# Differential queries' transpose stored and loaded from ScalarE's queue, head outputs reloaded one step later

## What is computed

```python
for l in range(2):
    h = rms_norm(x, norm_gain)
    proj = h @ w_in                       # q, k, v, z of both kinds, and two gates
    # 8 differential heads (DA): q, k are normed and rotated first
    a  = softmax(mask(q1 @ k1.T)) - lam * softmax(mask(q2 @ k2.T))
    ua = rms_norm(a @ va) * (1 - lambda_init) * silu(da_z)
    # 16 stick-breaking heads (SB), two at a time
    w  = exp(log_sigmoid(z) + after)      # after: a reversed cumulative sum
    ub = (w @ vs) * silu(sb_z)
    y  = sigmoid(gate_a) * (ua @ w_branch_a) + sigmoid(gate_b) * (ub @ w_branch_b)
    x  = x + y @ w_out
x = second_block(x, ...)                  # two more layers, not touched here
```

## Time and profile before

| what | us |
|---|---|
| median of 3 runs | 3225.98 |
| range of the runs | 3220.62 to 3230.3 |
| the profiled execution, its own time | 3236.04 |
| span of its instructions | 3234.3 |
| PE busy | 3181.7 |
| DVE busy | 2051.8 |
| ACT busy | 1668.3 |

### The profile page before, as it was taken

The page is one execution under the profiler, slowest core; times in us unless marked ns, Lnnn a source line. Parts: engine busy times, 40 slices in busy tenths (PEclk is TensorE's granted clock), DMA queues, the critical chain, the costliest instruction groups (busy, mean ns, idle before and its releaser), DMA issues.

```text
span 3234.3 us, 46398 instructions
## 1 busy us (share of the span) xinstructions
PE 3181.7 (98%) x16602; PEld 2725.8 (84%) x16602; DVE 2051.8 (63%) x2347; ACT 1668.3 (52%) x2326; POOL 516.5 (16%) x425
## 2 busy tenths in 40 slices
PE   9999999999999999999999999999999999999999
PEld 7877878887888888778778888888889999999997
DVE  6766755555544455666655555544458888688975
ACT  5444455565444444454455555544446557465663
POOL 4635500000000003446420000000001000200000
PEclk9999999999999999999999999999999999999999
DMA  7656566666555555666566666665564444544454
GB/s 254 206 192 204 188 213 215 201 203 213 191 193 195 192 194 190 207 205 204 197 205 206 207 203 204 200 194 194 193 209 161 162 141 148 180 162 161 147 180 146
DMA packets 203372, 619.32 MB, mean 191 GB/s; under 512 B 22672, under 2 KB 57632, under 8 KB 202848
## 3 DMA queue, kind: packets, MB, share of 16 engines
q1 hardware_dynamic: 201760, 608.35, 58.1%
q0 software_dynamic: 1488, 9.26, 0.8%
HBM read 590.26 MB, written 27.26 MB: 191 GB/s over the span
## 4 chain that ended last, share of the span: by engine, by line
PE 73%; DMA 12%; DVE 5%; issue 4%; ACT 3%; SPq 3%; POOL 1%; ACTq 0%; DVEq 0%; POOLq 0%
PE acc L2042 15%; PE acc L2044 15%; PE acc L2043 15%; PE acc L2399 5%; PE acc L2400 5%; PE acc L2401 5%; DMA qk_moved<-QB 4%; DMA u_moved<-UB 4%; DMA UT<-u_moved 2%; DVE w_lo L1249 2%; DMA QL<-qk_moved 2%; ACT w_hi L732 2%; SPq L485 1%; DVE QB L1378 1%; SPq L495 1%
## 5 line engine op out<-in xcount | busy, mean ns | idle before, releaser
L1249 DVE TENSOR_TENSOR w_lo<-raw,w_hi 128x1024 fp32r<-128x1024 f32 x1055 | 1378.2, 1317 | 936.4 <-ACT w_hi L732 801.0
L732 ACT ACTIVATE w_hi<-raw 128x1024 fp32r<-128x1024 f32 x831 | 869.8, 1056 | 831.6 <-PE acc L2044 811.0
L2042 PE MATMUL acc<-w_hi,hT_hi 128*128 128x512 f32 x2560 | 1012.7, 396 | 13.7 <-DVE w_lo L1249 12.2
L2043 PE MATMUL acc<-w_lo,hT_hi 128*128 128x512 f32 x2560 | 999.3, 390 | 0.0
L2044 PE MATMUL acc<-w_hi,hT_lo 128*128 128x512 f32 x2560 | 999.2, 390 | 0.0
L2042 PEld LDWEIGHTS acc<-w_hi,hT_hi 128*128 128x128 f32 x2560 | 482.7, 189 | 117.9 <-DVE w_lo L1249 16.0
L2044 PEld LDWEIGHTS acc<-w_hi,hT_lo 128*128 128x128 f32 x2560 | 482.3, 188 | 102.4
L2043 PEld LDWEIGHTS acc<-w_lo,hT_hi 128*128 128x128 f32 x2560 | 482.9, 189 | 97.3
L746 ACT ACTIVATE w_hi<-raw 128x1024 fp32r<-128x1024 f32 x224 | 236.1, 1056 | 260.3 <-PE acc L2401 200.3
L2399 PE MATMUL acc<-h_hi,w_hi 128*128 128x272 f32 (+1 forms) x1088 | 318.5, 293 | 0.0
L2400 PE MATMUL acc<-h_lo,w_hi 128*128 128x272 f32 (+1 forms) x1088 | 311.9, 287 | 0.0
(11 more groups left out here) (377 smaller groups left out, 3764.3 us busy)
## 6 DMA issues: line engine op xcount, KB each, us to landing
raw<-weights SPq DMA_DIRECT2D x1056, 512.0 KB, 4.0
qk_moved<-QB SPq DMA_DIRECT2D x32, 512.0 KB, 4.3
QL<-qk_moved SPq DMA_DIRECT2D x128, 128.0 KB, 3.1
u_moved<-UB SPq DMA_DIRECT2D x32, 256.0 KB, 3.7
UT<-u_moved SPq DMA_DIRECT2D x128, 64.0 KB, 2.6
mat<-mats POOLq DMA_DIRECT2D x2, 1536.0 KB, 8.8
X<-x_in SPq DMA_DIRECT2D x8, 256.0 KB, 7.6
GB_rows<-rows POOLq DMA_DIRECT2D x1, 2048.0 KB, 10.8
```

The source lines that it names most:

```text
L732: act.activation(w_hi[:, slot, :], raw[:, slot, :], ACT.Copy).then_inc(hi_ready, 1)
L1249: dve.tensor_tensor(w_lo[:, s % RING, :], raw[:, s % RING, :], w_hi[:, s % RING, :], ALU.subtract)\
L2042: pe.matmul(o, stat[0][:, kc, token], hi, start=(kc == 0), stop=False)
L2043: pe.matmul(o, stat[0][:, kc, token], lo, start=False, stop=False)
```

## The change

Three things change.

1. For DA heads, the store to `qk_moved` and the loads into `QL` are issued by ACT and no more by SP. On ACT the store stands behind half 3, `evac_vz` follows, and the four loads stand between it and half 4. DVE's transpose into `QB` moves ahead of half 1 (it stood ahead of half 2).
2. For SB pairs, the store and the loads stay on SP. The four loads into `QL` move from behind half 16's weight load to the end of the step.
3. The output of a head is still stored in the step in which it is made, but its four loads into `UT`, `u_hi` and `u_lo` move into the following step: on SP behind the weight load of half 7, on ACT behind half 4, on DVE behind half 5. A step therefore gets a third argument, `done`, the head before `prev`, and the first loop turn of each kind is written out. The last head of a layer is handled behind the steps.

```diff
-                step(kind_of(l, i, "SB"), kind_of(l, i - 1, "SB"))
-            step(None, kind_of(l, 7, "SB"))
+                step(kind_of(l, i, "SB"), kind_of(l, i - 1, "SB"), kind_of(l, i - 2, "SB"))
+            step(None, kind_of(l, 7, "SB"), kind_of(l, 6, "SB"))
...
+        def load_qk(eng, m):
+            eng.wait_ge(qk_stored, 16 * (m["n"] + 1))
+            for j in range(4):
+                eng.dma_start(QL[32 * j:32 * j + 32, :, :, :].rearrange("p i b r -> p i (b r)"),
...
# SP
-                loads(first, 4, 6)
-                if prev["kind"] == "DA":
-                    store_qk(prev)
-                loads(first, 6, 7)
-                if prev["kind"] == "DA":
-                    load_qkT(prev)
-                loads(first, 7, 16)
+                loads(first, 4, 8)
+                if done:
+                    load_uT(done)
+                loads(first, 8, 16)
                 if this and this["kind"] == "SB":
-                    store_qk(this)
-                loads(first, 16, 17)
+                    store_qk(sp, this)
+                loads(first, 16, 17 + late)
+                store_u(prev)
+                loads(first, 17 + late, 20)
                 if this and this["kind"] == "SB":
-                    load_qkT(this)
-                loads(first, 17, 17 + late)
-                store_u(prev)
-                loads(first, 17 + late, 18 + late)
-                load_uT(prev)
-                loads(first, 18 + late, 20)
+                    load_qk(sp, this)
...
# ACT
-                if prev:
-                    split(u, 0, 4)
-                    evac_vz(prev)
+                split(u, 0, 4)
                 if prev["kind"] == "DA":
-                    split(u, 4, 6)
+                    store_qk(act, prev)
+                evac_vz(prev)
+                if prev["kind"] == "DA":
+                    load_qk(act, prev)
+                split(u, 4, 5)
+                if done:
+                    u_hi(done)
+                if prev["kind"] == "DA":
+                    split(u, 5, 6)
                     copy_qkT(prev)
...
                 split(u, 12, 16)
-                u_hi(prev)
...
# DVE
-                split(u, 0, 2)
+                split(u, 0, 1)
                 if not late:
                     turn_qk(prev)
-                split(u, 2, 7)
+                split(u, 1, 6)
+                if done:
+                    u_lo(done)
+                split(u, 6, 7)
...
                 split(u, 13 + late, 16)
-                if prev:
-                    u_lo(prev)
```

More of the change, by code:

```diff
@@ L440, in layer_steps, with store_qk @@
             first(kind_of(l, 0, "DA"))
[L441 to L444, removed]
-                step(kind_of(l, i, "SB"), kind_of(l, i - 1, "SB"))
-            step(None, kind_of(l, 7, "SB"))
+            step(kind_of(l, 1, "DA"), kind_of(l, 0, "DA"), None)
+            with eng.Fori(2, 8) as i:
+                step(kind_of(l, i, "DA"), kind_of(l, i - 1, "DA"), kind_of(l, i - 2, "DA"))
+            step(kind_of(l, 0, "SB"), kind_of(l, 7, "DA"), kind_of(l, 6, "DA"))
+            step(kind_of(l, 1, "SB"), kind_of(l, 0, "SB"), kind_of(l, 7, "DA"))
+            with eng.Fori(2, 8) as i:
+                step(kind_of(l, i, "SB"), kind_of(l, i - 1, "SB"), kind_of(l, i - 2, "SB"))
+            step(None, kind_of(l, 7, "SB"), kind_of(l, 6, "SB"))
+        def store_qk(eng, m):
+            eng.wait_ge(qk_blocks, m["n"] + 1)
+            eng.dma_start(qk_moved.rearrange("i c j n -> (i c) j n"), QB[:, :, :, :].rearrange("p j b r -> p j (b r)")).then_inc(qk_stored, 16)
+        def load_qk(eng, m):
+            eng.wait_ge(qk_stored, 16 * (m["n"] + 1))
+            for j in range(4):
+                eng.dma_start(QL[32 * j:32 * j + 32, :, :, :].rearrange("p i b r -> p i (b r)"),
+                              qk_moved[:, :, j, :].rearrange("i c n -> c i n")).then_inc(qk_loaded, 16)
         def first_unit(this, prev):
@@ L476, in loads @@
                       .then_inc(raw_loaded[slot], 16)
[L478 to L486, removed]
             def store_u(m):
@@ L500, in first_step, with step @@
                 loads(first, RING, 16 + RING)
-            def step(this, prev):
+            def step(this, prev, done):
                 first = HALVES * first_unit(this, prev)
                 late = 1 if prev["kind"] == "SB" else 0
-                loads(first, 4, 6)
-                if prev["kind"] == "DA":
-                    store_qk(prev)
-                loads(first, 6, 7)
-                if prev["kind"] == "DA":
-                    load_qkT(prev)
-                loads(first, 7, 16)
+                loads(first, 4, 8)
+                if done:
+                    load_uT(done)
+                loads(first, 8, 16)
                 if this and this["kind"] == "SB":
-                    store_qk(this)
-                loads(first, 16, 17)
+                    store_qk(sp, this)
+                loads(first, 16, 17 + late)
+                store_u(prev)
+                loads(first, 17 + late, 20)
                 if this and this["kind"] == "SB":
-                    load_qkT(this)
-                loads(first, 17, 17 + late)
-                store_u(prev)
-                loads(first, 17 + late, 18 + late)
-                load_uT(prev)
-                loads(first, 18 + late, 20)
+                    load_qk(sp, this)
             for l in range(DEPTH):
@@ L525, in _ @@
                 first = HALVES * (UNITS1 * l + 2 * HEADS + 2) + RING
+                loads(first, 0, RING)
+                load_uT(kind_of(l, 7, "SB"))
                 rest = HALVES * UNITS1 * (l + 1) + (RING if l + 1 < DEPTH else HALVES2 * DEPTH) - first
                 assert rest % RING == 0
-                with sp.Fori(0, rest // RING) as r:
+                with sp.Fori(1, rest // RING) as r:
                     loads(RING * r + first, 0, RING)
@@ L867, in step @@
                 else:
-                    split(u, 4, 5)
                     copy_qkT(prev)
@@ L915, in _ @@
                 evac_gate(l, 0, 1)
-                split(g0 + 2, 4, 16)
+                split(g0 + 2, 4, 6)
+                u_hi(kind_of(l, 7, "SB"))
+                split(g0 + 2, 6, 16)
                 with act.Fori(1, 3) as j:
@@ L1452, in _ @@
                 g0 = UNITS1 * l + 2 * HEADS
-                split(g0 + 2, 0, 12)
+                split(g0 + 2, 0, 7)
+                u_lo(kind_of(l, 7, "SB"))
+                split(g0 + 2, 7, 12)
                 branch(l, 0, 0)
```

## The result

The changed kernel takes **3358.33 us** (median of 4 runs, 3352.81 to 3360.34), the kernel before 3228.14 beside it (4 runs): ratio **1.040**, 95% interval 1.038 to 1.042. That is 4% slower, well outside the range of 3200 to 3260.

A forecast was written before the change was run, and what follows sets the result against it. PE was taken to bound the kernel, busy 3181.7 of 3234.3 us. -12.0 + 23.2 - 1.6 - 3 = +6.6 on the profiled 3236.0 gave 3242.6, or 3233 us as a median; range for 8 in 10: 3200 to 3260.

The forecast's parts named there:

- The `w_lo` wait at SB starts: PE's waits for the first `w_lo` at the start of SB steps go, halves 0 to 2 being rounded earlier: -12.0 us.
- The SB step: PE waits 1.45 us before each SB pair's scores, `QT` standing behind `u_hi` on ACT: +23.2 us.
- Transpose and store of the DA step: In DA steps the transpose ends 0.8 us after half 0 and the store leaves at 1.4, 1.0 us earlier.
- The flight of `QL` and `UT` in a DA step: In DA steps `QL` loads land after 4.41 to 5.96 us, and `UT` takes 4.75 from first issue to `u_hi`.
- the crowding rival: Stores, `QL`, `UT` and unheld weight loads meet early in DA steps: 3.0 us a DA step, +46 us, 3272; chance 0.14.
- `QT` behind `u_hi`: On ACT in DA steps `QT` follows `u_hi` and half 5; PE waits 1.9 us, 30.4 against 32.0: -1.6 us.
- The clock: Four stretches of halved clock after long PE waits, in place of six times 3.4 us: -3 us.
- the loads land early: `UT` takes 3.38 us, SB waits vanish, DA waits fall to 0.3 us a step: -49 us, median 3177; chance 0.21.

The follow-up runs named there:

- e10: Changed kernel with the weight loads of halves 4 to 7 cut to 256 KB in place of 512, result wrong by intention: 3262.8 us, ratio 1.010.
- e7: Changed kernel, but in DA steps with `done` SP holds three `UT` loads and weights from half 7 until `QL` lands; `u_hi`, `u_lo` behind softmax: 3221.1 us.
- e11: Changed kernel with `u_hi` moved behind `QT` on ACT and `u_lo` one half later on DVE, all DMAs unchanged: 3293.0 us, ratio 1.018.
- e3: Changed kernel with `UT` loaded ahead of the step's first weight load: 3282.3 us, ratio 1.017.
- e6: e3 with the four `QL` loads issued by SP behind half 7's weight load, store still on ACT: 3272.1 us, ratio 1.015.
- e12: Changed kernel, but every DA step holds SP's weight loads from half 6 until `QL` lands; mask, mix, softmax ahead of held halves: 3173.9 us, ratio 0.983.
- e9: e5 with the transpose behind half 1, as it was before the change: 3184.4 us, ratio 0.986.
- e5: e3 with the DA store and `QL` loads back on SP in their old places, transpose still ahead of half 1: 3244.8 us, ratio 1.005.

## Why the prediction was wrong

By its own steps, in the spans (forecast +6.6, measured +116.7):

- **The `w_lo` wait at SB starts**: -12.0 forecast, gone. Right.
- **The SB step**: 1.45 us a step forecast, 29.4 / 16 = 1.84 measured, inside the bounds of 0.1 to 1.9. The mechanism was right; the term that was small is `UT`, 5.2 us from first issue to last landing where 4.75 was taken. +6.2 us.
- **Transpose and store of the DA step**: right within 0.35 us up to the store's issue. The store then took 2.76 us, not 4.30: with the early transpose no weight load leaves ahead of it. This error was to the good and was lost again.
- **The flight of `QL` and `UT` in a DA step** is the step that failed. The prediction took 4.41 to 5.96 us for `QL` and 4.75 for `UT`, all from steps of the kernel before, and they took 10.2 and 9.8. Those durations belonged to an order in which SP stood waiting, for `QB` and for the store, with the weight loads queued behind it. The prediction put 0.7 us on that and named against the crowding rival that "the same bytes move in the same stretch today". They do (in the first 13 us of a DA step 3.4 MB before and 3.0 in the changed kernel, by the packets of the traces), but not in front of `QL`: before, one weight load left beside the store and the next four behind `QL`, as the rows below show. e10 and e7 show the price: 2.3 and 2.8 us for each 512 KB of weights that leaves beside `QL`.

SP's issues in the step of the kernel before that starts at 151.73:

```profile
154.15 0.33 SPq L480 DMA_DIRECT2D qk_moved<-QB  x1
155.40 0.33 SPq L475 DMA_DIRECT2D raw<-weights  x1
158.46 1.76 SPq L485 DMA_DIRECT2D QL<-qk_moved  x4
160.43 7.88 SPq L475 DMA_DIRECT2D raw<-weights  x4
```

- **`QT` behind `u_hi`**: the chain of the forecast, and it held. By e11 the order costs 65 us, since ACT waits out the later of two late loads and then rounds two more operations. DA waits: 99.6 against 30.4 forecast, +69.2 us.
- **The clock**: -3 forecast, +31.6 measured, +34.6. It follows from the steps above; waits near 2 us cost little, since of the 16 SB waits, 1.8 us on average, six have a stretch at 0.50, of 3.4 us each, which is about 10 us in all. What was missing is that DA waits near 6 us cost again in the clock, here 37% of the added waits in PE's busy time (31.6 / 84.8).

The three errors make 6.2 + 69.2 + 34.6 = 110.0, and with the forecast 116.6 of the 116.7 us. The rival "the transfers crowd" had the right mechanism at about a third of its size: +46 us for the +130 of the medians, and 3.0 us a DA step for the 6.2 measured. The rival "the loads land early" rested partly on the rule of the Trainium skill ("DMA: Bandwidth & Descriptors", section "Queues, rings and completion order") that `QL` on a ring of its own takes turns with the weight packets instead of standing behind them. No run shows a gain from that: e3, with its own ring, lands `QL` 0.45 us later than e6, which stands in line. In the step above, the changed kernel's q10 moves no packet from 169.23 to 171.60, the first 2.4 us behind `QL`'s issue, while q1 moves 0.83 MB of weights. Why taking turns gave no head start stays open.

Open stays why a stall sometimes leaves the clock alone; no run was made on it. Open is also why a weight load beside `QL` costs more than its bytes at the rate of the full stretch.

## What to carry to other kernels

A wait in a queue that issues bulk loads can be what protects a short, urgent transfer. Before removing or moving such a wait, count the bytes that it lets loose and divide them by the rate of the busiest stretch of the trace (here 2.36 MB by 271 GB/s, 8.7 us): that, and not the landing time read in the old order, is the least that the new landing takes. It was 10.2 us here, since loads that leave during the flight count too. Make the throttle explicit where it is wanted, as e12 does, and put non-urgent data (`UT`) at the head of a step and its consumer behind the urgent one.

## What the runs showed of the hardware

- The DMA engines together gave 276 GB/s in a stretch with a share of 0.82 and 271 in one with 1.01, so the share alone doesn't tell what is left. Averaged over the flights of `QL` in DA steps it was 254 GB/s in the changed kernel and 243 before.
- The same store of 512 KB took 2.8 us with no weight load ahead of it (2.76 on ACT in the changed kernel, 2.81 on SP in e9) and 4.4 to 5.3 us behind one (on average 4.40 in the DA steps before and 5.28 in e5, both on SP): the company counts, not the issuing engine.
- POOL's last `QN` operation took 1.90 us in all 16 DA steps of the changed kernel, where DVE stands idle for it, and 2.23 to 2.76 in those of the kernel before, where DVE mostly worked beside it. POOL's timeline of the changed kernel:

```profile
163.25 1.90 POOL L602 TENSOR_TENSOR QN<-QN,small 128x1024 f32<-128x1024 f32 x1
```
